# Scaled rows between two decoder layers turned by DMA and VectorE instead of TensorE

## The reference, cut to what matters

```python
for i in range(DEPTH):                      # DEPTH = 2
    h = _rms_norm(x, pre_norm[i])           # x / rms(x) * g, row by row
    proj = h @ w_in[i]                      # columns: mixer, memory queries, gate
    ...                                     # layer 0: short gated conv; layer 1: differential attention
    mem_n = _rms_norm(mem, mem_norm[i])
    cross_out = _memory_cross_attention(q_mem, mem_n, w_kv_mem[i])
    branch = concatenate([tok_out, cross_out]) * silu(gate)
    y = branch @ w_out[i]
    x = x + _rms_norm(y, post_norm[i])
```

## Time and profile before

| | |
|---|---|
| median of 3 runs | 963.57 us (959.42 to 963.98) |
| the profiled execution, whole | 964.46 us |
| its span, first to last instruction | 962.7 us |
| PE busy | 947.7 us, 98% |
| DVE busy | 630.4 us, 65% |
| ACT busy | 475.4 us, 49% |
| DMA, mean rate | 189 GB/s |
| granted TensorE clock, mean | 0.997 |

### The profile page before, as it was taken

One profiled execution on the slowest core, in us unless ns is written; L12 is line 12 of the kernel. 1 busy time (PEld: TensorE's weight loads), 2 busy tenths in 40 slices (PEclk: granted clock), 3 DMA queues, 4 the chain that ended last, 5 costly groups with the idle time before them and its releaser, 6 DMA issues.

```text
span 962.7 us, 14077 instructions
## 1 busy us (share of the span) xinstructions
PE 947.7 (98%) x5148; PEld 813.1 (84%) x5148; DVE 630.4 (65%) x867; ACT 475.4 (49%) x725; POOL 1.2 (0%) x9
## 2 busy tenths in 40 slices
PE   8899999999999999999999999999999999999996
PEld 7788888888888888888888888888888888888885
DVE  5677666656665656645596447457778878886555
ACT  6756634344434343344465445445465465554441
POOL 0000000000000000000000000000000000000000
PEclk9999999999999999999999999999999999999998
DMA  9657555666666656655666655565655765646562
GB/s 330 203 171 260 174 176 178 191 191 192 189 191 181 189 179 191 205 192 194 199 203 201 183 169 179 171 197 167 205 167 162 219 184 164 200 148 203 192 196 89
DMA packets 148762, 182.31 MB, mean 189 GB/s; under 512 B 8112, under 2 KB 116976, under 8 KB 147952
## 3 DMA queue, kind: packets, MB, share of 16 engines
q1 hardware_dynamic: 147776, 177.25, 59.2%
q10 hardware_dynamic: 944, 4.49, 1.2%
HBM read 176.48 MB, written 2.10 MB: 185 GB/s over the span
## 4 chain that ended last, share of the span: by engine, by line
PE 95%; DMA 2%; DVE 1%; ACT 0%; SPq 0%; issue 0%; DVEq 0%; ACTq 0%
PE psum L368 40%; PE psum L369 20%; PE psum L428 10%; PE psum L430 10%; PE psum L429 10%; DMA stage_area<-in_mem_dram 1%; PE psum L604 1%; PE psum L447 1%; PE psum L472 1%; PE psum L455 1%; DMA raw_ring<-in_w_kv_mem_dram 1%; DVE lo_ring L914 1%; PE psum L576 0%; PE psum L464 0%; ACT hi_ring L653 0%; PE psum L586 0%
## 5 line engine op out<-in xcount | busy, mean ns | idle before, releaser
L368 PE MATMUL psum<-hT_split,hi_ring 128*128 128x512 f32 x1600 | 564.4, 398 | 0.0
L914 DVE TENSOR_TENSOR lo_ring<-raw_ring,hi_ring 128x1024 fp32r<-128x1024 f32 x319 | 386.1, 1223 | 256.8 <-ACT hi_ring L653 255.0
L653 ACT ACTIVATE hi_ring<-raw_ring 128x1024 fp32r<-128x1024 f32 x319 | 336.4, 1062 | 398.1 <-PE psum L369 262.0
L369 PE MATMUL psum<-hT_split,lo_ring 128*128 128x256 f32 x1600 | 447.2, 279 | 0.0
L368 PEld LDWEIGHTS psum<-hT_split,hi_ring 128*128 128x128 f32 x1600 | 300.3, 188 | 72.8 <-issue 2.0
L369 PEld LDWEIGHTS psum<-hT_split,lo_ring 128*128 128x128 f32 x1600 | 301.7, 189 | 0.1
L428 PE MATMUL psum<-hi_ring,branchT_split 128*128 128x512 f32 x256 | 99.9, 390 | 0.0
L430 PE MATMUL psum<-hi_ring,branchT_split 128*128 128x512 f32 x256 | 99.6, 389 | 0.0
L429 PE MATMUL psum<-lo_ring,branchT_split 128*128 128x512 f32 x256 | 99.6, 389 | 0.0
L430 PEld LDWEIGHTS psum<-hi_ring,branchT_split 128*128 128x128 f32 x256 | 48.1, 188 | 10.1
L429 PEld LDWEIGHTS psum<-lo_ring,branchT_split 128*128 128x128 f32 x256 | 48.1, 188 | 10.0
(11 more groups left out here) (186 smaller groups left out, 671.8 us busy)
## 6 DMA issues: line engine op xcount, KB each, us to landing
raw_ring<-in_w_in_dram SPq DMA_DIRECT2D x224, 512.0 KB, 4.5
raw_ring<-in_w_out_dram SPq DMA_DIRECT2D x64, 512.0 KB, 4.9
raw_ring<-in_w_kv_mem_dram SPq DMA_DIRECT2D x31, 512.0 KB, 4.6
layer_area<-layer_area SPq DMA_DIRECT2D x48, 64.0 KB, 3.2
stage_area<-in_mem_dram SPq DMA_DIRECT2D x8, 256.0 KB, 7.1
x_residual<-in_x_dram SPq DMA_DIRECT2D x2, 1024.0 KB, 9.7
x_residual<-in_x_dram ACTq DMA_DIRECT2D x1, 2048.0 KB, 10.1
layer_area<-in_post_norm_dram ACTq DMA_DIRECT2D x2, 1024.0 KB, 5.4
```

Of the source, the lines that this page charges most:

```text
L368: mm(o, hi[:, k, P * c:P * (c + 1)], X[:, kt, :], start=kt == 0, stop=False)
L369: last = mm(o[:, SEQ:], lo[:, k, P * c:P * (c + 1)], X[:, kt, 0:SEQ], start=False, stop=kt == KT - 1)
L653: run(whi[:, slot, :], raw[:, slot, :], ACT.Copy).then_inc(hi_ready, 1)
L914: V_.tensor_tensor(wlo[:, slot, :], raw[:, slot, :], whi[:, slot, :].bitcast(f32), SUB)\
```

## The change

PE no longer turns the rows of layer 1. The scaled rows `y_all` (two token tiles of 128 tokens by 2048) are cut into blocks of 32 tokens by 32 features. Thirty-two transfers inside SBUF (`to_quad`) carry the blocks to where each lies on the 32 partitions that its features are to have, still unturned: `quads`. DVE then turns each 32x32 block in place with its own transpose (`turn_quads`, 4 instructions for each token tile) into `h1T`, and ACT and DVE make the high and low halves of XA from it (`turned_h1`, from SBUF instead of PSUM). `quads` and `h1T` lie in the area of XC, which is free between the two layers.

One transfer is one (token tile t, token block tb, feature block b): 32 partitions by 16 tiles by 32 floats, so 512 pieces of 128 bytes, 64 KB in all. SP issues the 16 of token blocks 0 and 1, ACT the 16 of token blocks 2 and 3; each waits for the scaling of its token tile. In SP's list they stand three ahead of each of the loads of units 172, 173, 174 and 175 and two ahead of each of 176 and 177. In ACT's list they stand three ahead of the `high` of unit 171, three ahead of each of 172, 173 and 174, and four ahead of 175. DVE's `turn_quads(0)` stands ahead of the `low` of unit 175 and `turn_quads(1)` ahead of 177; each waits for all 16 transfers of its token tile. `turned_h1` stands, on ACT, half ahead of the `high` of unit 177 and half ahead of 178; on DVE, half ahead of the `low` of unit 178 and half ahead of 179.

To have the rows earlier, the squares of token tile 0 move ahead of the `high` of unit 167, and `scale_h1` moves ahead of the `low` of unit 168.

```diff
+    quads = nc.alloc_sbuf_tensor_at("h1_quads", [P, KT, SEQ // 32, 32], f32, offset=xc_at).ap()
+    h1T = nc.alloc_sbuf_tensor_at("h1_turned", [P, KT, SEQ], f32, offset=xc_at + 4 * KT * SEQ).ap()
...
+    def to_quad(q, loaded, t, tb, b):
+
+        to = quads[32 * b:32 * b + 32, :, 4 * t + tb, :]
+        rows = y_all[32 * tb:32 * tb + 32, t, :].rearrange("r (k b c) -> r k b c", k=KT, b=4)[:, :, b, :]
+        q.dma_start(to, rows).then_inc(loaded[t], 16)
+
+    SP_QUADS = [(t, tb, b) for t in range(TT) for tb in range(2) for b in range(4)]
+    ACT_QUADS = [(t, tb, b) for t in range(TT) for tb in range(2, 4) for b in range(4)]
...
+        def sp_quads(first, n):
+            for t, tb, b in SP_QUADS[first:first + n]:
+                sp.wait_ge(xs_ready, TT + 1 + t)
+                to_quad(sp, sp_quads_loaded, t, tb, b)
...
-            row_group(u + 2 * B_UNITS, w_kv_mem[l], CROSS_WIDTH, in_order)
+            row_group(u + 2 * B_UNITS, w_kv_mem[l], CROSS_WIDTH, in_order,
+                      at={n: lambda n=n: sp_quads(3 * (n - 4), 3) for n in range(4, 8)} if l else {})
...
-            column_group(U_QM1 + B_UNITS * i, w_in[1], QM_COL + BCOLS * i)
+            column_group(U_QM1 + B_UNITS * i, w_in[1], QM_COL + BCOLS * i,
+                         at={n: lambda n=n: sp_quads(12 + 2 * n, 2) for n in range(2)} if i == 0 else {})
...
-        row_group(G_VM1, U_VM1, G_VM1 % 2, XB, in_order,
-                  at={1: turns_of(N_H1, range(4), y_all, lambda: pe.wait_ge(xs_ready, 4)),
-                      4: turns_of(N_H1, range(4, 8), y_all)})
+        row_group(G_VM1, U_VM1, G_VM1 % 2, XB, in_order)
...
+        def turned_h1(n):
+
+            act.wait_ge(h1_turned, 4 + n // 2 + 1)
+            for kt in (2 * n, 2 * n + 1):
+                last = run(XA[:, kt, 0:256], h1T[:, kt, :], ACT.Copy, scale=gT[:, KT + kt:KT + kt + 1])
+            last.then_inc(tr_hi, 1)
...
-        column_group(G_KM1, U_KM1, G_KM1 % 2)
-        for t in range(TT):
+        def new_squares(t):
             act.wait_ge(x_new, t + 1)
             squares(xres[:, t, :], y_all[:, t, :], ss[:, 2 + t:3 + t], x_squared)
+
+        column_group(G_KM1, U_KM1, G_KM1 % 2, at={3: lambda: new_squares(0)})
+        new_squares(1)
...
-        column_group(G_KM1 + 1, U_KM1 + B_UNITS, (G_KM1 + 1) % 2)
+        def act_quads(first, n):
+            for t, tb, b in ACT_QUADS[first:first + n]:
+                act.wait_ge(xs_ready, TT + 1 + t)
+                to_quad(act, act_quads_loaded, t, tb, b)
+
+        column_group(G_KM1 + 1, U_KM1 + B_UNITS, (G_KM1 + 1) % 2, at={3: lambda: act_quads(0, 3)})
         row_group(G_VM1, U_VM1, G_VM1 % 2, vm, scale=mem_rstd,
-                  at={1: steps_of(N_H1, range(4), XA, KT), 4: steps_of(N_H1, range(4, 8), XA, KT)})
+                  at={0: lambda: act_quads(3, 3), 1: lambda: act_quads(6, 3), 2: lambda: act_quads(9, 3),
+                      3: lambda: act_quads(12, 4), 5: lambda: [turned_h1(n) for n in range(4)],
+                      6: lambda: [turned_h1(n) for n in range(4, 8)]})
...
-                     at={2: scale_h1})
+                     at={0: scale_h1})
...
-        row_group(U_VM1, at={1: steps_of(N_H1, range(4), XA, KT), 4: steps_of(N_H1, range(4, 8), XA, KT)})
+        def turn_quads(t):
+
+            dve.wait_ge(sp_quads_loaded[t], 16 * 8)
+            dve.wait_ge(act_quads_loaded[t], 16 * 8)
+            for c in range(4):
+                V_.transpose(h1T[:, 4 * c:4 * c + 4, P * t:P * (t + 1)], quads[:, 4 * c:4 * c + 4, 4 * t:4 * t + 4, :])\
+                  .then_inc(h1_turned, 1)
+
+        def turned_h1(n):
+
+            dve.wait_ge(tr_hi, N_H1 + n + 1)
+            for kt in (2 * n, 2 * n + 1):
+                last = V_.scalar_tensor_tensor(XA[:, kt, 256:512], h1T[:, kt, :], gT[:, KT + kt:KT + kt + 1],
+                                               XA[:, kt, 0:256].bitcast(f32), MULT, SUB)
+            last.then_inc(tr_lo, 1)
+
+        row_group(U_VM1, at={3: lambda: turn_quads(0), 5: lambda: turn_quads(1),
+                             6: lambda: [turned_h1(n) for n in range(4)], 7: lambda: [turned_h1(n) for n in range(4, 8)]})
```

More of the change, by code:

```diff
@@ L202, in build @@
     xs_ready = sem("xs_ready")
+    sp_quads_loaded, act_quads_loaded = ([sem(f"{q}_quads_loaded{t}") for t in range(TT)] for q in ("sp", "act"))
+    h1_turned = sem("h1_turned")
     angle_ready, table_ready = sem("angle_ready"), sem("table_ready")
@@ L236, in column_group, with row_group @@
                      w[:, B_KT * n:B_KT * (n + 1), bass.ds(col, BCOLS)])
-        def row_group(u, w, col, order):
+        def row_group(u, w, col, order, at={}):
             w = w.rearrange("(k p) n -> p k n", p=P)
             for n, k in enumerate(order):
+                if n in at:
+                    at[n]()
                 unit(u + n, n % SLOTS, raw[:, n % SLOTS, :].rearrange("p (k c) -> p k c", k=A_KT),
```

## The result

The changed kernel takes 968.58 us (median of 12 executions, 965.66 to 974.11), the kernel before 964.18 us (12 executions, 959.42 to 965.25). The ratio is 1.0053 [1.0031, 1.0075]: slower, by about the 0.5% that the prediction named as the limit of a measurement. The ranges leave no doubt of the direction: the fastest of the 12 executions, 965.66 us, is above the slowest of all 95 executions of the kernel before that are on record, 965.51 us. The forecast was 970.0 us.

What follows compares the result with a forecast made beforehand. PE was taken to bound the kernel, busy 98% of the span. -3.5 (PE) + 8.9 (wait for unit 176) + 1 (issue) = +6.4 us, 970.9 from the profiled execution, 970.0 for the median; range 962.5 to 983.

Steps and rivals of the forecast that it cites:

- The limit of 3.5 us: On PE: removing 32 transposes saves 3.5 us, 0.36% of the time, the most that can be gained.
- The front: Around units 167 and 168: earlier squares and scale_h1 cost nothing; if DVE is 0.3 us later, PE waits 0.3 us.
- The chain with free transfers: Turned rows through DVE and ACT to unit 176: PE waits 2.4 us even with free transfers, leaving a 1.1 us gain.
- The packet: DMA engines: a 128-byte packet costs 14 ns, so a transfer 0.46 us and all 32 together 14.7 us of every engine.
- What the packet decides: Rival, transfers nearly hidden if below some 0.33 us each: PE waits 2.4 to 5 us, -1.1 to +2 us; chance 0.22.
- the prediction's sum: DMA work ahead of the load of unit 176: 21.7 us from 496, including 26 transfers, so it lands at 518.2.
- The wait ahead of unit 176: On PE: ready at 519.9, remainders done at 528.8, so it waits 8.9 us; less 3.5, +5.4 us.
- The issue term, +1 us,: On ACT: a blocked issue stands ahead of the high; 1 us added, with 0 and 5 us as ends.
- the rival: ACT blocked by its own issues: five bursts of 1 to 2 us add +5 to +9 us, 975 to 980; chance 0.13.
- on SP a blocked issue only keeps the order: SP's queue: blocked issues given no cost there, whereas on ACT they stand ahead of the high.
- The clock: On PE: sum wrong if TensorE's granted clock, 1.00, fell to its lower level after so long a wait; no size given.
- Dear packets: Rival: 32 partitions serving 16 engines make packets cost 28 ns, +18 us, 982; at 52 ns over 1000; chance 0.13.

Runs made afterwards that it cites:

- e8: Kernel before with only the two moves to the front (squares of tile 0, scale_h1): 964.24 us in one profile, seam +0.1 us.
- e4: Kernel before, PE's transposes kept and used, with the 32 transfers and the moves to the front added: 963.91 us, ratio 0.9999.
- e2: Changed kernel without its 32 transfers, DVE transposing straight from y_all, so the output is wrong: 964.15 us, ratio 0.9989.
- e3: Changed kernel, each transfer moving one 2 KB run per partition, still 32 partitions to 32, output wrong: 966.88 us, ratio 1.0042.
- e5: Changed kernel, each transfer going over all 128 partitions in runs of 512 bytes, output wrong: 963.87 us in one profile, seam +3.9 us.
- e6: Changed kernel with DVE's first remainders ahead of the low of unit 177, the second half ahead of 178: 967.21 us, ratio 1.0044.
- e7: Changed kernel with e6's move, blocks turned in place first, then 32 transfers in 2 KB runs; scale_keys(1) three units later: 967.1 us, ratio 1.0038.
- e11: e7 with 24 transfers, eight blocks kept on their partitions and copied by GpSimd, DVE's second turn one unit earlier: 959.35 us, ratio 0.9976.
- e9: Changed kernel with 66 unused transposes of the identity on PE ahead of unit 176, filling its wait: 970.45 us, ratio 1.0064.

## Why the prediction was right

Point by point, in the order of its steps.

**The limit of 3.5 us** was right: PE has the 32 transposes less, and no version gained more than 1.4 us.

**The front** was right: e8 and e4 moved the seam by 0.1 and 0.0 us.

**The chain with free transfers** was right within 0.3 us: forecast a wait of 2.4 us and -1.1, measured 2.1 and -1.2 in e2. The transpose, taken at 0.65 us, is 2.49 / 4 = 0.62:

```profile
515.41 2.49 DVE L1234 STREAM_TRANSPOSE h_turned<-h_quads 128x512 f32<-128x512 f32 x4
```

**The packet** was right: forecast 14 ns from the line through the earlier trace rows, measured 13.7.

**What the packet decides** was wrong, and here the forecast had luck. By the prediction the transfers are hidden below some 0.33 us of each engine's time for a transfer. In e3 a transfer costs 66 / 16 / 16 = 0.26 us, and the prediction's sum (9.7 + 26 x 0.26 = 16.5 us from 496) lets the load of unit 176 land 29 us after the first `add_y`; it landed after 34.2, and PE waited 7.7 us. The sum keeps the weights at their price of before and lets the engines do one thing at a time. Neither held: the weight packets became a third dearer, and the engines' share was 1.25. In the changed kernel the two seem to cancel, and the landing is met within 1 us (35.0 against 35.8); with longer pieces it isn't.

The rule of the Trainium skill in "DMA: Bandwidth & Descriptors", "Why small descriptors are slow (HBM only)", that transfers between SBUF and SBUF don't suffer from small pieces, is not borne out: the same megabyte took 111 us of the engines in pieces of 128 bytes and 66 in pieces of 2 KB. The 78% that this section of the Trainium skill gives is of a remote transfer, which no run here has. The rule in "Issuing engines are not separate DMA queues" of the same page of the Trainium skill, that all transfers run on the same 16 engines, agrees with the trace: the shares of q1 and q10 add up to 1.24, and q1's weight packets took 123 ns instead of 89 beside q10's. What the second issuing engine saved no run shows.

**The wait ahead of unit 176** was forecast at 8.9 us. Measured: 7.8, and 0.9 ahead of unit 175, together 8.7. (The prediction's landing has a slip of its own: 496 + 21.7 is 517.7, not 518.2, which makes the wait 8.4.) The forecast put the landing of the load of 176 at 518.2 and PE's start at 528.8; shifted by the 5.9 us between the two profiled executions, that is 512.3 and 522.9. The chain above has 513.1 and 523.3. Unit 175 was said to just hold, and didn't, by 0.9 us: its load was put at 515 and landed at 510.0 + 5.9 = 515.9.

**The issue term, +1 us,** stands for something that cost next to no time here. The issues did get slower (ns min/median/max):

```profile
L230 SPq DMA_DIRECT2D h_quads<-stage_area x16: 591/708/2574, 489.7 to 507.2; - x16
L230 ACTq DMA_DIRECT2D h_quads<-stage_area x16: 593/722/2232, 491.9 to 509.0; - x16
```

and ACT was blocked by them, as the rival says:

```profile
498.14 3.64 ACTq L230 DMA_DIRECT2D h_quads<-stage_area  x3
501.88 1.06 ACT L675 ACTIVATE hi_ring<-raw_ring 128x1024 fp32r<-128x1024 f32 x1 [2.71 <-DMA raw_ring<-in_w_kv_mem_dram]
...
506.26 3.80 ACTq L230 DMA_DIRECT2D h_quads<-stage_area  x4
510.17 1.06 ACT L675 ACTIVATE hi_ring<-raw_ring 128x1024 fp32r<-128x1024 f32 x1 [2.85 <-DMA raw_ring<-in_w_kv_mem_dram]
```

The three issues end at 501.78 and the `high` starts at 501.88; the four end at 510.06 and the `high` starts at 510.17. Four of the five bursts ended 0.1 us before the next `high`, although the trace names a load as its releaser. But the loads of units 172 to 175 landed at 497.74, 501.82, 506.23 and 510.01, the bursts ahead of their `high` ended at 498.01, 501.78, 505.45 and 510.06. So the blocked issues held up the `high` of 172 by 0.3 us and the others by 0.1 or less, and the rival's +5 to +9 didn't come on top. That loads and issues end together shows that its argument against, that bursts drain between units, was wrong. Likewise "on SP a blocked issue only keeps the order" was too easy: SP issued nearly without a pause from 489.65 to 509.86, and in the chain its issues are 14 us long. e3, where they are short and PE waits as long, shows that they are not a second cause.

**The clock** was the named risk, and it came: 0.61 on average over 8 us, 1.4 us lost, which by luck fills the place of the issue term. So the sum, +6.4 against 6.9 measured in the seam, is right partly by exchange: without its issue term and with the measured clock it would be +6.8.

**From the seam to the median.** Group against group the change costs some 7 us (from 959.42, or 958.2 to 960.4 in the later series, to 966; from 964.2 to 971). The medians differ by 4.4 us only, where 6.4 were forecast, since 11 of 12 executions of the kernel before and about half of those of the changed one were in the slower group. That the median of 968.6 comes within 1.4 us of the forecast is partly this mix. The executions of the changed kernel at 967.7 and at 973 to 974 us fit neither group; what sets the mix, and these, isn't known.

**Dear packets** didn't occur at 28 ns. But its argument, that a quarter of the partitions serves all 16 engines, was half right, for the price of the weights beside the transfers (e3 and e5 above) and for the transfers themselves: 1 MB over all partitions took 55 us in pieces of 512 bytes, over 32 of them 66 us, although its pieces were 2 KB long.

## What to carry to other kernels

Work taken off the engine that bounds a kernel is worth only what the step that replaces it leaves: list the new chain through every in-order list with its start times, first with free transfers (here 1.2 of 3.5 us), then with them. Late weights that a ring absorbs cost nothing (e4), while a step that stands in the same list behind a late weight inherits its delay in full, so put it ahead of the next weight's work (e6, 4.3 us). Count for a transfer not only its own time but what it does to the traffic beside it (weights a third dearer beside transfers over 32 partitions, e3; little over 128, e5). To transpose first, so that the blocks move in long runs, was no gain by itself (e7 is no better than e6); together with fewer transfers, blocks kept at home and an earlier start it gave the one version whose seam is shorter than before with all of the work done (e11).

## What the runs showed of the hardware

A transfer inside SBUF in pieces of 128 bytes costs 13.7 ns per packet; 1 MB takes 111 us of the engines' time, in pieces of 2 KB 66 us, over 128 partitions in pieces of 512 bytes 55 us, each beside a stream of weights. A weight packet of 2 KB took 89 ns before, 121 to 123 ns beside transfers over 32 partitions, 97 ns beside transfers over 128.

An issue of such a transfer took 0.59 to 2.57 us with 512 pieces of 128 bytes, and 0.51 to 0.77 us with 32 pieces of 2 KB. A compute instruction that runs already goes on beside an issue; the next one on ACT started 0.1 us after the last issue ahead of it (501.88, 510.17).

The granted clock fell after waits of PE of 4.1 to 7.8 us (0.50 over 520 to 524 us in the changed kernel and in e5), and not after waits of 2.1 us or less, with one exception: in e9's profile it fell after 1.9 us behind 66 transposes of 128 columns. The loss was 1.4 to 2.9 us of PE's time, not proportional to the wait (2.9 after 5.1, 1.4 after 7.8). All this is of the profiled executions: four of the ten of e2 have a mean granted clock of 0.994 or 0.995, the profiled one 0.997, so behind its wait of 2.1 us it may fall at times.

One and the same program runs its mixer loop at 115 or 117 matmuls in 20 us, at a granted clock of 1.00 in both and without a wait of PE. Over the kernel this is some 5 us. No run here settles why.
